# Chunked delta rule scan on one core: stored k k' products, values corrected by k times the state, a respread substitution

## What is computed

```python
# S_t = exp(g_t) (I - beta_t k_t k_t^T) S_{t-1} + beta_t k_t v_t^T,  o_t = S_t^T q_t
A = jnp.where(strict, jnp.einsum('nbhid,nbhjd->nbhij', kb, kc) * decay, 0.0)
rhs = jnp.concatenate([vc * bc[..., None], kb * jnp.exp(G)[..., None]], axis=-1)
sol = lax.linalg.triangular_solve(A + jnp.eye(CHUNK), rhs, lower=True, unit_diagonal=True)
u, w = sol[..., :dv], sol[..., dv:]
def step(S, xs):
    v_new = u_c - jnp.einsum('bhck,bhkv->bhcv', w_c, S)
    o = q_c @ S + qk_c @ v_new
    S = gl * S + k_c^T @ v_new
```

## Time and profile before

| | us |
|---|---|
| median of 3 runs (4896.88 to 4900.69) | 4899.91 |
| the profiled execution, its own time | 4903.0 |
| its span | 4901.2 |
| PE busy in the span | 4418.5 (90%) |
| DVE busy | 2321.5 (47%) |
| ACT busy | 1401.9 (29%) |
| POOL busy | 979.6 (20%) |
| chain that ended last: PE's part | 61% |

### The profile page before, as it was taken

How to read it: one execution, slowest core, us unless ns; L and a number is a source line. 1 busy time by engine, 2 the same in 40 slices (tenths; PEclk the granted TensorE clock), 3 DMA queues, 4 the chain that set the end, 5 groups by cost and what they waited for, 6 DMA issues and landing times.

```text
span 4901.2 us, 45672 instructions
## 1 busy us (share of the span) xinstructions
PE 4418.5 (90%) x18432; PEld 3071.2 (63%) x18432; DVE 2321.5 (47%) x3691; ACT 1401.9 (29%) x2623; POOL 979.6 (20%) x761
## 2 busy tenths in 40 slices
PE   7895788988899999998889998989888978999998
PEld 3454774665688888745554455554564647888886
DVE  2777755333466563336350116572676644333334
ACT  2452222112211111332321004351463532222222
POOL 0114443230244442006151000001000011000001
PEclk9996899999999999897989999999999999999999
DMA  5111133112243342111111110102000021111111
GB/s 185 39 30 53 52 116 101 52 52 77 65 116 112 108 116 63 68 46 51 52 43 43 35 44 20 31 24 86 18 22 15 18 97 49 52 45 44 46 49 60
DMA packets 249299, 293.63 MB, mean 60 GB/s; under 512 B 18513, under 2 KB 209377, under 8 KB 247553
## 3 DMA queue, kind: packets, MB, share of 16 engines
q1 hardware_dynamic: 230656, 208.80, 14.0%
q0 software_dynamic: 15312, 76.68, 4.9%
q10 hardware_dynamic: 3120, 5.24, 0.3%
HBM read 263.22 MB, written 27.47 MB: 59 GB/s over the span
## 4 chain that ended last, share of the span: by engine, by line
PE 61%; DVE 9%; ACT 5%; DMA 1%; issue 1%; POOL 1%; SPq 0%; POOLq 0%; DVEq 0%; ACTq 0%
PE bank L193 59%; PE bank L196 2%; DVE Mx L205 1%; ACT Mx L202 1%; ACT at21P L202 1%; ACT at20P L202 1%; DVE at21sm L223 1%; POOL sq L205 1%; DVE at20sm L223 1%; DVE x L211 0%; DMA wslot<-in_w_in 0%; DVE wfl L205 0%; DVE at11sm L223 0%; DMA hT<-hspill 0%; DMA wslot<-in_w_out 0%
## 5 line engine op out<-in xcount | busy, mean ns | idle before, releaser
L193 PE MATMUL bank<-h,wslot 128*128 128x512 f32 (+3 forms) x2096 | 896.1, 571 | 32.6 <-DMA wslot<-in_w_in 18.9
L193 PEld LDWEIGHTS bank<-h,wslot 128*128 128x128 f32 (+1 forms) x2096 | 381.9, 190 | 377.0 <-issue 359.9
L193 PE MATMUL bank<-hT,wslot 128*128 128x512 f32 (+3 forms) x1136 | 465.5, 567 | 36.7 <-DMA hT<-hspill 20.2
L193 PEld LDWEIGHTS bank<-hT,wslot 128*128 128x128 f32 (+1 forms) x1136 | 213.4, 191 | 264.4 <-issue 237.4
L193 PE MATMUL bank<-ffn1h,wfh 128*128 128x512 f32 x704 | 279.8, 398 | 12.0 <-DVE ffn1l L211 11.1
L193 PE MATMUL bank<-ffn2h,wgh 128*128 128x512 f32 x704 | 276.5, 393 | 9.6 <-DVE ffn2l L211 9.2
L211 DVE SCALAR_TENSOR_TENSOR x<-bank,mod,x 128x512 f32<-128x512 f32 x224 | 164.4, 746 | 248.0 <-PE bank L193 247.6
L193 PE MATMUL bank<-ffn1l,wfh 128*128 128x512 f32 x704 | 275.1, 391 | 0.0
L193 PE MATMUL bank<-ffn2l,wgh 128*128 128x512 f32 x704 | 274.8, 390 | 0.0
L193 PE MATMUL bank<-ffn1h,wfl 128*128 128x512 f32 x704 | 274.7, 390 | 0.0
L193 PE MATMUL bank<-ffn2h,wgl 128*128 128x512 f32 x704 | 274.7, 390 | 0.0
(11 more groups left out here) (536 smaller groups left out, 8995.7 us busy)
## 6 DMA issues: line engine op xcount, KB each, us to landing
wslot<-in_w_in SPq DMA_DIRECT2D x40, 1024.0 KB, 5.6
ffn1t<-in_w_mod POOLq DMA_DIRECT2D x64, 512.0 KB, 4.8
wslot<-in_w_ffn_in SPq DMA_DIRECT2D x44, 512.0 KB, 5.3
Mx<-acsT SPq DMA_DIRECT2D x32, 512.0 KB, 4.8
at1w<-in_ada_w POOLq DMA_DIRECT2D x24, 512.0 KB, 4.8
wslot<-in_ffn_w_gate SPq DMA_DIRECT2D x22, 512.0 KB, 4.0
wslot<-in_ffn_w_up SPq DMA_DIRECT2D x22, 512.0 KB, 5.3
hT<-hspill POOLq DMA_DIRECT2D x2, 5120.0 KB, 15.4
```

Of the source, the lines that this page charges most:

```text
L193: return Counted() if counting[0] else self.q.matmul(o, l, r, start=start, stop=stop)
```

## The change

1. **k k' kept.** `kk_act` gets one more ACT copy of the whole bank to `E[n % 2]`, waiting from the third chunk on until the store of two before has landed; SP stores it to the new tensor `kks` (256 KB each, ten of them). In the scan SP loads it straight into `kkE` (20 loads), PE's group `k` is gone, and DVE multiplies kkE, now in SBUF, by E in place.
2. **Values from k times the state.** The groups `nw` and nw * S, ACT's copy of `nw` and POOL's kb * bG are gone. A group `ks` (k times S) is new at the head of a step, and `rest` on DVE (four `stt` for each direction) adds it, times -beta exp(G), to vb. `vn` is then one group, and comes after `pt(s+1)`.
3. **Order.** `st` comes after `v1(s+1)` on PE and DVE. The rings have six and two banks.
4. **Early rows.** The gate rows of steps 0 and 1 are loaded in the preparation, to the buffers of the reciprocals; ACT computes E of step 0 before it waits for the preparation's end; SP no longer waits for the stored v before its first loads.
5. **The substitution's spread.** Batch 1 starts at s = 0 and batch 2 at s = 2; at the start four pieces, then `more(2)` where s < 2 and `more(1)` after.

```diff
     def kk_act(e, c):
...
+        n = KKS.index(c)
+        if n >= 2:
+            e.wait_ge(*kk_out[n % 2].after(n - 2))
+        e.activation(E[n % 2][:, :], b[:, :], AF.Copy).then_inc(gs.act("kk", c), 1)
         bk_p.give(("kk", c), gs.act.now())
+    def kk_sp(e, n):
+        c = KKS[n]
+        e.wait_ge(*gs.act.after("kk", c))
+        e.dma_start(io["kks"][c * 128:(c + 1) * 128, :], E[n % 2][:, :]).then_inc(kk_out[n % 2](n), 16)
     def gp_sp(e):
...
-        for g in (4, 5):
-            load(e, ("qkv", g), [(w1, 0, 8, g * 256, 256, 0)])
+        load(e, ("qkv", 4), [(w1, 0, 8, 4 * 256, 256, 0)])
+        for n in range(5):
+            kk_sp(e, n)
+        load(e, ("qkv", 5), [(w1, 0, 8, 5 * 256, 256, 0)])
+        for n in range(5, 8):
+            kk_sp(e, n)
+        e.wait_ge(*gc_out.after("out"))
+        e.wait_ge(*gp.pool.after("unit", 3, 512))
+        rows(e, 0)
+        rows(e, 1)
         for m in range(8, 12):
...
+            if m == 8:
+                kk_sp(e, 8)
+                kk_sp(e, 9)
-    bk_m, bk_b = Ring(bank[0:5]), Ring(bank[5:8])
+    bk_m, bk_b = Ring(bank[0:6]), Ring(bank[6:8])
     def gs_sp(e):
-        for ev in gp.ends() + [hs_out.after("out"), ks_out.after("out"), vs_out.after(11)]:
+        for ev in gp.ends() + [hs_out.after("out"), ks_out.after("out")]:
             e.wait_ge(*ev)
+        def kks(s):
+            for d in range(2):
+                c = order[d][s]
+                if s >= 2:
+                    e.wait_ge(*gs.pe.after("pt", s - 2, d))
+                e.dma_start(kkE[s % 2][d][:, :], io["kks"][c * 128:(c + 1) * 128, :]).then_inc(kk_in[s % 2](s, d), 16)
...
+        kks(0)
+        kks(1)
...
+        e.wait_ge(*vs_out.after(11))
         for s in range(10):
             chunk(s)
             if 1 <= s < 9:
-                rows(s + 1)
+                rows(e, s + 1)
+                kks(s + 1)
     def gs_pe(e):
+        def ks(s):
+            for d in range(2):
+                b = bk_m.take("ks", s, d)
...
+                e.wait_ge(*gs.dve.after("S", s - 1, d))
+                for x in range(4):
+                    i = e.matmul(b[:, hs[x]], kch(s, d, x), St[(s - 1) % 2][d][:, hs[x]])
+                i.then_inc(gs.pe("ks", s, d), 1)
         for s in range(10):
...
+            if s:
+                ks(s)
             if s < 9:
                 pt(s + 1)
+            for d in range(2):
+                e.wait_ge(*gs.dve.after("u", s, d))
+                e.wait_ge(*(gs.dve.after("r", s, d) if s else gs.pool.after("vb", s, d)))
+                four("vn", s, d, Va[d], vb[d])
+            if s < 9:
+                v1(s + 1)
                 for d in range(2):
                     e.wait_ge(*gs.pool.after("kd", s, d))
                     e.wait_ge(*gs.act.after("vn", s, d))
                     four("st", s, d, kd[d], vn[d])
-                v1(s + 1)
     def gs_act(e):
+        for i in range(2):
+            e.wait_ge(*kk_out[i].after(8 + i))
         begin(0)
+        barrier(e, gp)
+        e.wait_ge(*hs_out.after("out"))
         begin(1)
     def gs_dve(e):
-                e.tensor_tensor(kkE[s % 2][d][:, :], bk_b["k", s, d][:, :], E[d][:, :], OP.mult).then_inc(gs.dve("kkE", s, d), 1)
+                e.tensor_tensor(kkE[s % 2][d][:, :], kkE[s % 2][d][:, :], E[d][:, :], OP.mult).then_inc(gs.dve("kkE", s, d), 1)
+        def rest(s, d):
+            b, col, o = bk_m["ks", s, d], gcol(s, d), vb[d]
+            e.wait_ge(*gs.pe.after("ks", s, d))
+            e.wait_ge(*gs.pool.after("vb", s, d))
+            for x in range(4):
+                e.stt(o[:, hs[x]], b[:, hs[x]], bG[:, col + x:col + x + 1], o[:, hs[x]],
+                      OP.mult, OP.add).then_inc(gs.dve(*(("r", s, d, x) if x < 3 else ("r", s, d))), 1)
         for s in range(10):
-            if s in (0, 3):
+            k = 2 if s < 2 else 1
+            if s in (0, 2):
+                more(41)
                 pieces = sub(e, 1 if s == 0 else 2)
+                more(4)
+            for d in range(2):
+                if s:
+                    rest(s, d)
```

More of the change, by code:

```diff
@@ L644, in build @@
     W0, gcr = rb("Wd0", [1024]), rb("gcr", [128])
+    rsts = Ring([rb(f"rst{i}", [TT]) for i in range(2)])
+    Gr = [[t[:, d * 512:(d + 1) * 512] for d in range(2)] for t in rsts.bufs]
+    kk_out, kk_in = ([Sem(f"{n}{i}", 16) for i in range(2)] for n in ("kko", "kki"))
     gc_out, gr_in = Sem("gcT", 16), [Sem(f"gr{i}", 16) for i in range(2)]
@@ L651, in build @@
     accs = Ring([sb(f"acc{i}", [1288]) for i in range(2)])
-    rsts = Ring([sb(f"rst{i}", [TT]) for i in range(2)])
     vtok = sb("vtok", [NC * 512])
@@ L1165, in begin @@
             for d in range(2):
-                b = bk_b.take("k", s, d)
-                for ev in bk_b.freed("k", s, d):
-                    e.wait_ge(*ev)
-                for x in range(4):
-                    i = e.matmul(b[:, hs[x]], kch(s, d, x), kch(s, d, x))
-                i.then_inc(gs.pe("k", s, d), 1)
                 if lat(s, d):
@@ L1262, in gs_pe @@
                 uu(s + 1)
-                new(s + 1)
     def gs_act(e):
-        barrier(e, gp)
-        e.wait_ge(*hs_out.after("out"))
         def begin(s):
@@ L1298, in gs_act @@
                 begin(s + 2)
-            if s < 9:
-                for d in range(2):
-                    e.wait_ge(*gs.pe.after("nw", s + 1, d))
-                    e.activation(nw[d][:, :], bk_m["nw", s + 1, d][:, :], AF.Copy, scale=-1.0).then_inc(gs.act("nw", s + 1, d), 1)
-                    bk_m.give(("nw", s + 1, d), gs.act.now())
     def gs_dve(e):
@@ L1335, in plus @@
             bk_m.give((name, s, d), gs.dve.now())
+        def rest(s, d):
[5 more added lines that the diff above has]
+                      OP.mult, OP.add).then_inc(gs.dve(*(("r", s, d, x) if x < 3 else ("r", s, d))), 1)
+            bk_m.give(("ks", s, d), gs.dve.now())
         def state(s, d):
@@ L1380, in gs_dve @@
                     pt(s + 1, d)
-                more(2)
+                more(k)
+            for d in range(2):
+                if s < 9:
+                    plus("v1", s + 1, d, Va)
+                more(k)
             for d in range(2):
@@ L1384, in gs_dve @@
                     state(s, d)
-                more(2)
-            for d in range(2):
-                if s < 9:
-                    plus("v1", s + 1, d, Va)
-                more(2)
+                more(k)
             for d in range(2):
                 y(s, d)
-                more(2)
+                more(k)
             for d in range(2):
@@ L4028 @@
         io[n] = nc.dram_tensor(n, (TT, 512), _mybir.dt.float32, kind="Internal").ap()
+    io["kks"] = nc.dram_tensor("kks", (TT, 512), _mybir.dt.float32, kind="Internal").ap()
     io["gcT"] = nc.dram_tensor("gcT", (80, 128), _mybir.dt.float32, kind="Internal").ap()
```

57 lines of the change are left out of this document (15 added, 42 removed).

## The result

The kernel after takes 4853.82 us, the median of four runs (4851.07 to 4855.87); four runs of the kernel before beside them gave 4899.76 (4896.88 to 4900.69). The ratio is 0.9908 with a 95% interval of 0.9892 to 0.9924: faster by 45.9 us. The forecast was 4878, its range 4860 to 4894, so the direction was right and the size was not: the gain is over twice the 21.5 us of the sum, and even the best of my rivals (40 us) stays short of it.

A forecast was written before the change was run, and what follows sets the result against it. It took DVE with waits to bound steps 0 to 4 and PE steps 5 to 7. 8.6 + 2.9 + 5 + 1.5 + 6.5 - 3.0 = 21.5 us off 4899.9 gave 4878, range 4860 to 4894.

The forecast's parts named there:

- the charge for waits for PE in steps 0 to 4: DVE still waits for PE at its low clock: 2.2 us a step in steps 2 to 4, 4.9 in steps 0 and 1.
- the surcharge on kkE: kkE with both operands in SBUF costs DVE 0.6 us more a time: 3.6 in steps 0 and 1, 3.6 in 2 to 4.
- Steps 2 to 4: Scan steps bound by DVE, with substitution: 109.2 us falls to 104.0, a gain of 5, bounds 1 and 11.
- Steps 0 and 1: First scan steps, bound by DVE: 81.7 us falls to 80.3, a gain of 1.5, bounds -4 and 7.
- Steps 5 to 7: PE-bound scan steps: two groups fewer net, 18.8 us a step, a gain of 8.6, bounds 3.7 and 10.8.
- The charge of 0.8 us a step: Steps 5 to 7: DVE's chain through rest ends late for vn, so a step takes 18.8 us instead of 18.0.
- Steps 8 and 9: Last scan steps, 27.39 us: gains of 1.8 in step 8 and 1.1 in step 9, together 2.9, bounds 0 and 3.6.
- The start and the preparation: Scan's start 6.5 us sooner (bounds 4 and 8); the preparation's copies make all that follows 3.0 later (bounds 0 and 6).
- The order: v1 ahead of st in the scan: Va comes sooner, the state later, wanted by ks only 9 us on; worth nothing.
- The waits vanish: Rival, chance 0.15: DVE meets no PE wait and POOL seldom, all upper bounds reached, a gain of 40 us: 4860.
- A DVE chain in the place of PE's work: Rival, chance 0.16: latency binds the scan's steps, removed matmuls return as waits; a gain of 8.5 us: 4891.
- The shared port decides: Rival, chance 0.09: DVE's row operations wait for POOL instructions, a batch costing 81 us in place of 47.3; slower: 4912.

The follow-up runs named there:

- Experiment 5: Kernel after with the group ks issued twice in each of steps 1 to 9, the second writing the same bank: 4858.6 us.
- experiment 8: Kernel after with the substitution's pieces of steps 1 to 4 moved behind the two pt, none behind v1, the state and the output: 4850.19 us.
- Experiments 7 and 3: Kernel after with part 4's loads moved back behind the stored v: 4858.75 us; kernel after with k k' computed again in the scan: 4859.7 us.
- experiment 12: Kernel after with st ahead of v1 again on PE, and the state ahead of Va on DVE: 4856.52 us.
- experiment 4: Kernel after with part 2 undone (nw, its copy, kb times bG, double vn ahead of pt) and the old st and v1 order: 4892.78 us, ratio 0.9988.
- experiment 11: Kernel after with early pieces (behind pt) in step 1 alone, and ten DVE copies given to ACT: 4849.76 us.

## Why the prediction was right in its sign and wrong in its size

**The step that failed** is the charge for waits for PE in steps 0 to 4, where the trace shows 0.3 us of them. Having taken away the wait ahead of PT, I put new ones in: "the outputs and v2 will sometimes be late: 2.2 us a step", 6.5 us in steps 2 to 4, and 4.9 us left in steps 0 and 1. With it goes the surcharge on kkE in the same steps: 7.2 us, of which 1.0 came. Of the 24.4 us by which the sum fell short, 16.9 lie in steps 0 to 4 (6.5 predicted, 23.4 measured), 2.9 in steps 5 to 7, 1.3 in steps 8 and 9, 0.6 in the start with the preparation, and 2.7 behind the scan.

I argued the waits from PE's low clock in these stretches. The trace of after shows idle time of DVE of 2.8 and 3.3 us in the two windows, most of it the gaps between dependent row operations that my sum counts separately, and 0.3 us of waits for PE in all five steps. Experiment 5 adds a whole group on PE in each of steps 1 to 4, at a clock that is still mixed (0.79 and 0.89), and DVE's idle time stays the same. The low clock was a sign that PE had slack, and I had priced it as a danger. The slack has an end: with other places for the pieces (experiment 8) DVE idles 6.6 us more in steps 2 to 4, and waits for PE for 3.3 us there. That the charge was wrong holds for this spread of the pieces.

*Steps 2 to 4*: predicted 104.0, measured 95.1. The 6.5 us of waits were not there; the six kkE took 4.06 us, 0.68 each, so the 0.6 more a time that I charged (3.6) did not come either. It was a slip of the sum: 0.6 is the whole price of kkE with POOL idle, and the busy time I added it to already held kkE at 0.69. Against that the batch beside POOL was dearer, 51.6 us on tile ktok where I allowed 49.3. 104.0 - 6.5 - 3.6 + 2.3 = 96.2. *Steps 0 and 1*: 80.3 predicted, 72.5 measured. 4.9 us of waits not there, and the six kkE took 5.11 us, 1.0 above the price of before instead of 3.6; batch 1 at 45.88 was as reckoned (47.32 less 1.6). 80.3 - 4.9 - 2.6 = 72.8.

*Steps 5 to 7*: 18.8 a step predicted, 17.82 measured: the two groups of PE with nothing charged against them, so the upper bound of 10.8 us was reached (11.5 by the stretch's ends, with a first step of 17.7). The charge of 0.8 us a step was the term that failed. The chain was sized wrong, not kkE: 6.54 us for six is 1.09 each, near the 1.3 I took. But I had added durations, 0.69 and 2.15 us, where starts are closer: QE starts at 586.16 and Va at 586.76, 0.60 on though QE takes 0.68, and kkE to the last QE is 3.4 us, not 4.0. Over the chain that makes 1.1 us, and the second `rest` ends before its group instead of after it. Durations of this view overlap between instructions in a row; a chain wants the differences of starts.

*Steps 8 and 9*: 2.9 predicted, 4.2 measured, beyond my bound of 3.6; which of their waits went I have not followed.

*The start and the preparation*: right in sum. First pt predicted 3.5 sooner than 395.79, measured 3.9. The rows of after:

```profile
305.84 6.56 DVE L217 RECIPROCAL rst<-rst 128x512 f32<-128x512 f32 x2 [6.05 <-ACT rst L202]
...
390.70 1.51 DVE L205 TENSOR_TENSOR kkE<-kkE,sq 128x512 f32<-128x512 f32 x2 [5.80 <-DMA kkE<-kks]
```

```profile
385.53 2.76 SPq L232 DMA_DIRECT2D kkE<-kks  x4
```

```profile
391.87 3.76 PE L193 MATMUL bank<-Dm,kkE 128*128 128x128 f32 x16 [9.89 <-DVE kkE L205]
```

The reciprocals of the earlier trace rows come 1.2 us later, where I had wanted some 3, but the last store of v goes from 382.25 to 384.93, 2.7 later (predicted 3.0), and SP's first load of the scan goes out at 385.53. The load is what DVE waits for. From the last store of v to kkE I had 6.6 us (0.4 to the first load, 0.9 to the second, 5.3 to kkE); it is 5.8. From kkE to pt I had 0.5, and it is 1.2. The two misses cancel nearly, which is luck. Experiments 7 and 3 show that both halves are there: without part 4's loads the first pt comes 8.3 later, without the stored k k' 6.0 sooner.

**The order** of st and v1, which I called worth nothing, is worth something between 0 and 5 us (experiment 12), with its cause open.

**The rivals.** "The waits vanish" was the nearest, with 0.15 of the chances. The half of its account that DVE meets no wait for PE held in steps 0 to 4; the other half, that it meets POOL seldom, did not, since batch 2 cost 51.6 us. I had put 40 us on it: steps 0 to 4 gained 23.4 where its bounds allowed 18 (they still carried the surcharge on kkE), while start and preparation together gave 4.1 where it had 8. "A DVE chain in the place of PE's work" did not occur: PE waits for `vb` in the steady steps once, 0.9 us. "The shared port decides" had its mechanism right and its price far too high: 1.3 us for nearly each of 62 row operations, 81 us for a batch. In the timelines of DVE and POOL of the kernel after, 29 of the 62 row operations of batch 2 begin while an instruction of POOL runs, which then has 0.9 us left on the average, 25.8 in all. In batch 1 it is 20 of them, and 18.8 us. Each of these 49 ends 0.04 to 0.29 us after that instruction of POOL, and none of the other 75 takes more than 0.43 us.

The page "SBUF — State Buffer" of the Trainium skill, section "SBUF: two separate sides", says that a vector operation with two SBUF inputs and a GpSimd operation that reads SBUF shut each other out for a whole instruction. The trace agrees, by these 49 operations. It agrees for kkE too: the second kkE above takes 1.42 us where it takes 0.68 with POOL idle, and ends 0.55 after POOL's Dm. The Dm beside it takes 1.99 where it takes 1.54 otherwise:

```profile
582.20 1.55 POOL L205 TENSOR_TENSOR DT<-ktok,cst 128x512 f32<-128x512 f32 x1
583.70 1.99 POOL L205 TENSOR_TENSOR Dm<-ktok,cst 128x512 f32<-128x512 f32 x1
```

A batch in the worst place seen (experiment 11) cost 55.6 us, against 31.2 with POOL at rest: POOL is idle there for 41 of 97.5 us, and the pieces that fall in that time are cheap.

**Which part brought what.** Part 2, with the order of st and v1, brings some 37 us of the scan (experiment 4; how much of it is the place of pt alone is open), and it is needed for the others: the spread is worth 9 us alone and 0.7 on top of it; stored k k' is worth 0.3 us a steady step without it (21.3 against 21.65) and 9.8 us over the scan's steps with it, of which it gives back 7.3 at the start. Part 4 brings 6.6. I had given the largest share to steps 5 to 7, where PE bounds and groups can be counted; the larger one came where an engine waited on a round trip.

## What to carry to other kernels

Where two engines wait for each other in turn, look up what is *issued* between the request and the answer: pt needed nothing from the vn group ahead of it. Moving it to the front of the step, together with the new form of the values, took away 46.6 us of waits for 19.4 us (nine times 2.15) of new vector work. When you take such a wait away, the stretch can become the sum of the other engine's instructions, as here. Don't add waits back only because an engine's clock is low; look for its idle time first. And gains of parts are not to be added: price each on the kernel without the others and on top of them.
